# Weight quarters of the first pass placed one quarter on, and two transposes of each expert moved ahead of its down product

## What is computed

```python
for e in range(N_EXPERTS):                      # 32 experts, D_MODEL = D_EXPERT = 1024
    g = jnp.minimum(t @ w_gate[e] + b_gate[e], SWIGLU_LIMIT)
    u = jnp.clip(t @ w_up[e] + b_up[e], -SWIGLU_LIMIT, SWIGLU_LIMIT)
    act = (u + 1.0) * (g * jax.nn.sigmoid(SWIGLU_ALPHA * g))
    out = out + comb[:, e:e + 1] * (act @ w_down[e] + b_down[e])
```

## Time and profile before

| | us |
|---|---|
| median of 3 runs | 1081.67 (1081.43 to 1082.17) |
| the profiled execution's own time | 1081.04 |
| its span, first to last instruction | 1079.2 |
| TensorE busy | 1040.2 |
| VectorE busy | 274.8 |
| ScalarE busy | 198.6 |

### The profile page before, as it was taken

The page is one execution under the profiler, slowest core; times in us unless marked ns, Lnnn a source line. Parts: engine busy times, 40 slices in busy tenths (PEclk is TensorE's granted clock), DMA queues, the critical chain, the costliest instruction groups (busy, mean ns, idle before and its releaser), DMA issues.

```text
span 1079.2 us, 12157 instructions
## 1 busy us (share of the span) xinstructions
PE 1040.2 (96%) x5114; PEld 445.0 (41%) x5114; DVE 274.8 (25%) x560; ACT 198.6 (18%) x347; POOL 29.5 (3%) x41
## 2 busy tenths in 40 slices
PE   9999999999999999999999999999999999999997
PEld 5889984333333333333333333333333333333332
DVE  6876753111111111111111111111111111111121
ACT  4657532111110111111111111111111001110111
POOL 0070020000000000000000000000000000000000
PEclk9999999999999999999999999999999999999999
DMA  9835999999999999999999999999999999999996
GB/s 316 302 104 179 387 390 383 394 428 427 434 431 428 438 428 431 427 437 432 430 430 431 436 430 432 428 437 431 431 430 432 435 430 432 422 428 429 427 425 275
DMA packets 37235, 433.75 MB, mean 402 GB/s; under 512 B 5030, under 2 KB 7627, under 8 KB 19659
## 3 DMA queue, kind: packets, MB, share of 16 engines
q1 hardware_dynamic: 36704, 432.64, 95.7%
q10 hardware_dynamic: 490, 0.56, 0.1%
HBM read 432.14 MB, written 1.05 MB: 401 GB/s over the span
## 4 chain that ended last, share of the span: by engine, by line
PE 76%; DMA 12%; ACT 6%; DVE 4%; issue 1%; SPq 0%; DVEq 0%
PE ps L1027 55%; DMA ring<-in_exp_w_up 11%; PE ps L932 5%; PE ps L979 5%; ACT arena L1336 3%; PE ps L679 2%; PE ps L681 2%; PE ps L680 2%; PE ps L1035 2%; DVE ring_r L1522 2%; PE ps L973 1%; DMA ring<-in_w_in 1%; ACT ring_r L1198 1%; ACT arena L1371 1%; PE ps L941 0%
## 5 line engine op out<-in xcount | busy, mean ns | idle before, releaser
L1027 PE MATMUL ps<-ring,arena 128*64 128x512 f32 x2432 | 538.4, 595 | 15.0 <-ACT arena L1371 11.3
L1027 PEld LDWEIGHTS ps<-ring,arena 128*64 128x64 f32 x2432 | 168.0, 137 | 339.0 <-issue 316.3
L1027 PE MATMUL ps<-arena 128*64 128x512 f32 x640 | 142.0, 595 | 5.0 <-ACT arena L1371 3.1
L1773 DVE TENSOR_TENSOR arena<-ps,gain 128x512 f32<-128x512 f32 x32 | 22.1, 692 | 275.6 <-PE ps L973 275.6
L1798 DVE TENSOR_SCALAR arena<-ps 128x512 f32<-128x512 f32 x30 | 20.8, 692 | 261.8 <-PE ps L1027 261.8
L1027 PEld LDWEIGHTS ps<-arena 128*64 128x64 f32 x640 | 44.4, 137 | 89.1 <-issue 85.2
L1336 ACT COPY arena<-ps 128x512 f32<-128x512 f32 x32 | 33.8, 1055 | 249.7 <-PE ps L932 249.7
L1375 ACT COPY arena<-ps 128x256 f32<-128x256 f32 x30 | 11.2, 372 | 293.3 <-PE ps L979 293.3
L1811 DVE TENSOR_SCALAR arena<-ps 128x512 f32<-128x512 f32 x31 | 21.4, 692 | 170.9 <-PE ps L1027 170.9
L979 PE MATMUL ps<-arena 64*128 64x512 f32 x256 | 63.9, 616 | 0.0
L932 PE MATMUL ps<-arena 128*64 128x512 f32 x256 | 60.6, 593 | 0.0
(11 more groups left out here) (231 smaller groups left out, 658.7 us busy)
## 6 DMA issues: line engine op xcount, KB each, us to landing
ring<-in_exp_w_up SPq DMA_DIRECT2D x19, 4096.0 KB, 29.3
ring<-in_exp_w_down SPq DMA_DIRECT2D x18, 4096.0 KB, 28.4
ring<-in_exp_w_gate SPq DMA_DIRECT2D x18, 4096.0 KB, 29.8
ring<-in_exp_w_down SPq DMA_DIRECT2D x12, 2048.0 KB, 39.1
ring<-in_exp_w_up SPq DMA_DIRECT2D x11, 2048.0 KB, 40.4
ring<-in_exp_w_gate SPq DMA_DIRECT2D x10, 2048.0 KB, 40.7
arena<-in_exp_w_gate SPq DMA_DIRECT2D x5, 4096.0 KB, 29.8
arena<-in_exp_w_down SPq DMA_DIRECT2D x5, 4096.0 KB, 30.4
```

The source lines that it names most:

```text
L1027: last = mm(ps[BLOCK * to:BLOCK * (to + 1), bank, :], src[:, c, half, :], moved, start=(fresh and half == 0 and c == 0), stop=(half == 1 a ...
L1773: v.tensor_tensor(h_in, ps[:, 6, :].rearrange("p (c h s) -> p c h s", c=4, h=2), wide(gain[:].rearrange("p h c -> p c h"), [P, 4, 2, BLOCK ...
```

## The change

**Placing.** In the first pass a matrix n from 5 to 14 is no longer placed on itself but one quarter further up: its quarter 0 goes to the last quarter of the place before (for n mod 5 = 1: to quarter 2 of `hold(0)`), its quarters 1, 2, 3 to the first three quarters of its own place. For 5 and 10 in `hold(0)` quarters 1, 2, 3 lie at 0, 1 and 3, and quarter 0 of 5 stays in `early_place`. The loads wait accordingly:

- Matrices 5 to 9, by quarters: quarter 2 of matrix 5 waits for the second quarter of matrix 0 and no longer for its third; each load behind it takes the wait of the quarter before.
- Matrix 10: quarter 0 waits for the end of matrix 4, the other three for the end of matrix 5, in two transfers (2 MB and 1 MB). Matrices 11 to 14: quarter 0 (1 MB) waits for the first half of matrix n - 5, the other three (3 MB, one transfer) for its end.
- In the rolled loop (matrices 15 to 74) each load waits for one half product more than before: the first half of matrix n - 4 instead of the end of matrix n - 5.

**Transposes.** A helper `turns` fixes the order between gather and down product: `turn_weights(5)` first, behind a new wait for VectorE's clamp, then `turn(7, act_out)`, then `turn(6, h_got)`, which so moves from behind the down product to before it. The last pair of experts uses the same helper.

```diff
         def halved(n, rolled=False):
-            return not rolled and (HOLDS <= n < PASS or n >= MATRICES * FINE)
+            return not rolled and (HOLDS <= n <= 2 * HOLDS or n >= MATRICES * FINE)
+
+        def moved_up(n, q):
+            if (n, q) == (HOLDS, 0):
+                return early_place
+            if n % HOLDS == 0 and q:
+                k, p = 0, (0, 1, 3)[q - 1]
+            elif q:
+                k, p = n % HOLDS, q - 1
+            else:
+                k, p = (n - 1) % HOLDS, 2 if n % HOLDS == 1 else 3
+            return hold(k)[:, p // 2, 2 * D * (p % 2):2 * D * (p % 2 + 1)]
...
-                if n >= HOLDS or not isinstance(base, int):
+                if not isinstance(base, int):
+                    sp.wait_ge(piece_done, of_round + both_halves + 1)
+                elif n >= HOLDS:
                     sp.wait_ge(piece_done, of_round + (first_half if halves else both_halves))
...
+                sp.wait_ge(piece_done, 2 * HOLDS)
+                sp.dma_start(moved_up(2 * HOLDS, 0), quarter_of(2 * HOLDS, 0)).then_inc(wrapped_in, 16)
+                sp.wait_ge(piece_done, 2 * HOLDS + 2)
+                sp.dma_start(hold_front[:, 0:4 * D], flat_rows(2 * HOLDS)[:, 2 * D:6 * D]).then_inc(matrix_in[0], 16)
+                sp.dma_start(moved_up(2 * HOLDS, 3), quarter_of(2 * HOLDS, 3)).then_inc(lower_in[0], 16)
+                for n in range(2 * HOLDS + 1, PASS):
+                    k = n % HOLDS
+                    sp.wait_ge(piece_done, 2 * (n - HOLDS) + 1)
+                    sp.dma_start(moved_up(n, 0), quarter_of(n, 0)).then_inc(quarter_in[k][0], 16)
+                    sp.wait_ge(piece_done, 2 * (n - HOLDS) + 2)
+                    sp.dma_start(hold(k).rearrange("p h x -> p (h x)")[:, 0:6 * D],
+                                 flat_rows(n)[:, 2 * D:]).then_inc(matrix_in[k], 16)
...
+            def turns(i):
+                pe.wait_ge(pick_ready, i + 2)
+                gather()
+                pe.wait_ge(expert_step, 2 * i + 2)
+                turn_weights(5)
+                pe.wait_ge(act_ready, i + 1)
+                turn(7, act_out).then_inc(act_T, 1)
+                pe.wait_ge(hg_ready, i + 2)
+                turn(6, h_got).then_inc(h_turned, 1)
...
                 gate_and_up(r, step, MATRICES * j, i, first)
-                pe.wait_ge(pick_ready, i + 2)
-                gather()
-                pe.wait_ge(act_ready, i + 1)
-                turn(7, act_out).then_inc(act_T, 1)
-                turn_weights(5)
+                turns(i)
                 pe.wait_ge(actT_ready, i + 1)
                 product(r, step, MATRICES * j + 2, 7, actT, fresh=True)
-                pe.wait_ge(hg_ready, i + 2)
-                turn(6, h_got).then_inc(h_turned, 1)
```

More of the change, by code:

```diff
@@ L364, in build @@
         last_quarter_in = sem("last_quarter_in")
+        wrapped_in = sem("wrapped_in")
         left_seats_in = sem("left_seats_in")
@@ L541, in by_halves, with quarter_of @@
                 return src.rearrange("p e h c n -> p h (e c n)")
+            def quarter_of(n, q):
+                return flat_rows(n)[:, 2 * D * q:2 * D * (q + 1)]
             def load_matrix(r, base, n):
@@ L584, in load_first_holds @@
                 sp.wait_ge(quarter_done, 1)
-                sp.dma_start(hold(0)[:, 0, 0:2 * D], first_down[:, 0, 2 * D:]).then_inc(matrix_in[0], 16)
-                sp.wait_ge(quarter_done, 2)
-                sp.dma_start(hold(0)[:, 1, 0:2 * D], first_down[:, 1, 0:2 * D]).then_inc(quarter_in[0][1], 16)
+                sp.dma_start(moved_up(HOLDS, 1), quarter_of(HOLDS, 1)).then_inc(matrix_in[0], 16)
+                sp.wait_ge(piece_done, 1)
+                sp.dma_start(moved_up(HOLDS, 2), quarter_of(HOLDS, 2)).then_inc(quarter_in[0][1], 16)
@@ new lines, in load_first_holds @@
+                    if k == 1:
+                        sp.wait_ge(quarter_done, 2)
+                    else:
+                        sp.wait_ge(piece_done, 2 * k)
+                    sp.dma_start(moved_up(n, 0), quarter_of(n, 0)).then_inc(quarter_in[k][0], 16)
+                    sp.wait_ge(quarter_done, 2 * k + 1)
+                    sp.dma_start(moved_up(n, 1), quarter_of(n, 1)).then_inc(matrix_in[k], 16)
+                    sp.wait_ge(piece_done, 2 * k + 1)
+                    sp.dma_start(moved_up(n, 2), quarter_of(n, 2)).then_inc(quarter_in[k][1], 16)
@@ new lines, in load_first_holds @@
+                    sp.wait_ge(quarter_done, 2 * k + 2)
+                    sp.dma_start(moved_up(n, 3), quarter_of(n, 3)).then_inc(lower_in[k], 16)
+                sp.wait_ge(piece_done, 2 * HOLDS)
[3 more added lines that the diff above has]
+                sp.dma_start(moved_up(2 * HOLDS, 3), quarter_of(2 * HOLDS, 3)).then_inc(lower_in[0], 16)
@@ L596, in load_round @@
+                for n in range(2 * HOLDS + 1, PASS):
+                    k = n % HOLDS
+                    sp.wait_ge(piece_done, 2 * (n - HOLDS) + 1)
+                    sp.dma_start(moved_up(n, 0), quarter_of(n, 0)).then_inc(quarter_in[k][0], 16)
+                    sp.wait_ge(piece_done, 2 * (n - HOLDS) + 2)
+                    sp.dma_start(hold(k).rearrange("p h x -> p (h x)")[:, 0:6 * D],
+                                 flat_rows(n)[:, 2 * D:]).then_inc(matrix_in[k], 16)
             def load_round(r):
-                for n in range(2 * HOLDS if isinstance(r, int) else HOLDS, PASS):
+                for n in range(PASS if isinstance(r, int) else HOLDS, PASS):
@@ L993, in product @@
                 first_pass = isinstance(r, int) and isinstance(step, int)
+                moved_on = first_pass and HOLDS <= n < 3 * HOLDS
                 by_quarters = first_pass and HOLDS <= n < 2 * HOLDS
@@ L1003, in product @@
                                     pe.wait_ge(landed, r * 16 + 16)
-                        if by_quarters and c == 0:
-                            pe.wait_ge(quarter_in[at][half], 16)
+                        if c == 0 and (by_quarters or moved_on and half == 0):
+                            pe.wait_ge(*((wrapped_in, 16) if n == 2 * HOLDS else (quarter_in[at][half], 16 * (n // HOLDS))))
                         if n == HOLDS - 1 and first_pass and half == 0 and c == 0:
@@ L1009, in product @@
                             pe.wait_ge(last_quarter_in, 16)
-                        if n not in TAIL and c == (2 if by_quarters else 0):
+                        if n not in TAIL and c == (2 if moved_on else 0):
                             if half == 0:
@@ L1019, in product @@
                             row = late_place[:, D * (c - 2):D * (c - 1)]
-                        elif n == HOLDS and first_pass and half == 0:
-                            row = early_place[:, D * c:D * (c + 1)] if c < 2 else hold_chunks(at)[:, 0, c - 2, :]
+                        elif moved_on:
+                            row = moved_up(n, 2 * half + c // 2)[:, D * (c % 2):D * (c % 2 + 1)]
                         for to in range(2):
```

## The result

The changed kernel takes 1085.8 us (median of 6 runs, 1085.33 to 1087.0), the kernel before 1081.74 us in the same comparison. The ratio is 1.0036, with a 95% interval of 1.0026 to 1.0047: slower, by 4.1 us where 3.7 had been forecast. The profiled execution took 1085.89 us (span 1084.1), so its span is 4.9 us longer than that of before.

What follows compares the result with a forecast made beforehand. The prediction took the weight stream to bound the kernel: the early lead is lost, matrix 15 lands 3.7 us late and the stream stays so, 1081.67 + 3.7 = 1085.4 us, range 1083.0 to 1087.5.

Steps and rivals of the forecast that it cites:

- The bound: Whole kernel: the weight stream ends it, the last up matrix has no slack, and TensorE's own gain turns into waiting.
- Rival E: Whole kernel: TensorE is the bound after all, 17.4 us less, 1064 us; chance 0.03.
- The lead of the quarters: Loads up to matrix 9, 180 to 205 us: earlier quarters win 3.0 us of the 3.4 lost there.
- Rival D: Queue at matrix 15: never empty there, so the lead of 3.0 us is kept, 1078.7 us; chance 0.08.
- TensorE's gain: Each expert's down product: the turn behind it moves to a covered place, saving TensorE 0.58 us an expert.
- rival B: Ahead of the down product: the moved turn delays it by what it saves behind, no gain, 1087.1 us; chance 0.09.
- Rival C: TensorE's short waits of 0.27 and 0.46 us go too, matrix 15 lands 2.2 us earlier, 1083.2 us; chance 0.10.
- The first hole: Matrix 10, around 230 us: the queue runs dry and 2.4 us of the 3.0 us lead are gone.
- The second hole: Matrix 15, around 281 us: issued at 278.99 behind an empty queue, landing at 293.1, 3.7 us later than before.
- the restart: What a transfer issued too late pays beyond its bytes: 4.35 us behind an empty queue, ends 3.15 and 5.45.
- rival C2: Matrix 15 behind the empty queue: a cheap restart of about 2 us, 1083.0 us; chance 0.04.

Runs made afterwards that it cites:

- late_quarter: The changed kernel, but of matrices 15 to 19 only the quarter whose place is still read waits longer, and the loop behind has the old wait: 1082.32 us.
- early_ten: The changed kernel with matrix 10's quarters loaded as their places come free, the loop's later wait kept: 1085.82 us.
- turns_only: The kernel before with the new order of the transposes alone, places and loads as they were: 1082.1 us, ratio 1.0002.
- the mended kernels: The changed kernel with matrix 10's quarters loaded earlier and the late wait at matrix 15 eased, without or with matrices 10 to 14 by quarters: 1080.29 and 1080.53 us.

## Why the prediction was right, and where it was not

**The bound.** Right. The stream ends the kernel: the transposes alone gain nothing, and the windows of the stream give the median of every kernel to within 0.7 us. Rival E is gone. As foreseen, TensorE now meets landings earlier, from 595 us on where it was 796, and waits up to 1.7 us and not 1.3.

**The lead of the quarters.** Right in size: 3.0 foreseen, 2.8 to 2.9 measured (420 to 422 GB/s for 372). Rival D, which keeps it to the end, fails at the two holes.

**TensorE's gain.** Mis-sized. The step took 0.58 us an expert and called the front of the down product free; it gives some 0.13 us back there. Gate products begin at 203.25, 230.60 and 257.95 us, 27.35 apart, where the kernel before has 27.8 (203.59 and 231.39). That is 0.45, so rival B's mechanism exists, at a quarter of its price. Rival C got nothing: of its two waits the 0.27 us for VectorE gave way to 0.22 us for ScalarE, and the 0.46 is what the moved transposes fill.

**The first hole.** Right in place and mechanism: 1.9 us at 230 where 2.4 were foreseen. What I had not seen is a second, smaller one at 240 to 243 us, 0.8 us: I wrote that matrices 11 to 14 follow in time, and matrix 11's three quarters, issued at the end of matrix 6 (237.73 us), do not. The sum left 0.6 us of the lead behind matrix 10; behind this second hole nothing is left of it. Window of the kernel before, then of the changed one:

```profile
240.00:243.00 3.00, 3.00 (x16) 1.01 (x14) 0.78 (x2) 0.00 (x0) 0.00 (x0) 1.00 1.03 437
240.00:243.00 3.00, 3.00 (x16) 1.01 (x14) 0.00 (x0) 0.00 (x0) 0.00 (x0) 1.00 1.04 322
```

**The second hole.** Right in place, wrong in two of its terms, which cancel in part. Matrix 15 was issued at 279.79 us and not 278.99: the 0.13 three times, about as much again ahead of matrix 11 itself, a down product, a first product 0.14 us later in this execution, and 0.16 us that the load in the rolled loop comes later behind its release (3.85 us behind the start of that product, 275.94, where late_quarter's load behind the same release comes 3.69 behind it). And the restart was not 4.35 us but 12.6 - 9.75 = 2.85 by matrix 15's landing, below the 3.15 that I had as its lower end; in the three other kernels with this hole (matrix 15 issued at 281.27, 281.11 and 279.75 us) the landings came after 12.2, 12.4 and 12.4 us.

By these two terms matrix 15 gives + 3.0, and the stream is 3.8 late. Matrix 16, issued at 289.00, landed 14.5 us later, at 303.5, which is 303.5 - (284.17 + 15.0) = 4.3 us later than before, though it met no empty queue: from 285 to 300 us the stream moves 435 GB/s (before: 433). So a landing is not the place of the stream, and the packets say by how much. When matrix 15 landed, the changed kernel had moved 0.37 MB less in all than the kernel before had at its own landing (97.28 and 97.65 MB): 0.9 us less was already under way behind it, and 3.0 + 0.9 is about what the stream had lost. At the landing of matrix 16 it is 0.17 MB more, and 4.3 - 0.4 is 3.9 again. The first landing behind a hole understates it. That the engines start together behind a hole and so finish closer together would explain it, but no view here tells them apart.

The restart of 4.35 so gave nearly the right end for a reason that I had not given: an issue forecast 0.8 us too early, and a cost of restart 1.5 us too high for the landing but near what the stream loses. That 1085.4 came so near 1085.8 is in part luck.

The page "DMA: Bandwidth & Descriptors" of the Trainium skill, section "Anatomy of one DMA", was nearer for matrix 15's own landing with its fixed 2.0 us, though it states them for GpSimd's path: an estimate of 11.75 us by it, 14.1 by my rows of the front part, 12.6 measured. The time worked out from it, 1083.0, failed all the same, and rival C2 with it.

## What to carry to other kernels

Before crediting a faster engine or an earlier load, ask what ends the kernel and look for the times at which its queue is empty: the bytes that the stream does not move in its windows gave the medians of nine kernels within 0.7 us. A wait that is one step later is free while the queue covers it, and at the first place where it does not, it can undo everything that was gained ahead of it, as in early_ten. So where a rotation of places is begun early to gain a lead, its end must be made as fine as its beginning: only the piece whose place is really taken may wait.

## What the runs showed of the hardware

In the changed kernel TensorE's clock fell three times in mid-stream to half its upper level (1.2 of 2.4 GHz) for 3.4 us, which it never did before the last microseconds of the kernel before. Window around one of them (PEclk is the column before the last two):

```profile
858.00:863.00 5.00, 5.00 (x18) 1.46 (x16) 0.00 (x0) 0.00 (x0) 0.00 (x0) 0.66 1.02 439
```

```profile
828.62 7.09 PE L1063 MATMUL ps<-arena 128*64 128x512 f32 x32 [1.71 <-DMA arena<-in_exp_w_up]
...
857.76 8.78 PE L1063 MATMUL ps<-ring,arena 128*64 128x512 f32 x32 [1.73 <-DMA ring<-in_exp_w_up]
...
886.90 7.09 PE L1063 MATMUL ps<-ring,arena 128*64 128x512 f32 x32
```

(TensorE's timeline around it.) The up product at 857.76 us begins after 1.73 us without work on TensorE, as the one at 828.62, but runs 8.78 us and not 7.09. The cost is hidden, since the up product of the expert behind it, at 886.90, then simply doesn't wait. turns_only, early_ten and the mended kernels show the same, two to four times each. The kernels with the old order of the transposes don't, and there no matmul waits for an expert's data longer than 1.3 us, where the new order has 1.7. That the longer wait makes the clock fall is inferred; it isn't enough by itself, since the clock stayed up behind the same wait at 828.62. In a kernel bound by TensorE each such product would cost 1.7 us.
